# Mixture-of-experts block on one core: two-block and one-block expert rounds take turns

## What is computed

```python
logits = hf @ w_router + b_router
top_vals, top_idx = lax.top_k(logits, 4)          # 1024 tokens, 32 experts
weights = softmax(top_vals)
...
def expert_block(args):                           # one block: up to 128 tokens of one expert
    x_i, e = args
    gu = x_i @ w_gate_up[e] + b_gate_up[e]        # 1024 -> 2048
    gate, up = jnp.split(gu, 2, axis=-1)
    gate = jnp.minimum(gate, 7.0)
    up = jnp.clip(up, -7.0, 7.0)
    act = (up + 1.0) * (gate * jax.nn.sigmoid(1.702 * gate))
    return act @ w_down[e] + b_down[e]            # 1024 -> 1024
```

## Time and profile before

| | |
|---|---|
| median of 3 runs | 3197.2 us (3193.49 to 3198.83) |
| the profiled execution | 3199.73 us, span 3198.2 us |
| TensorE matmul busy | 2709.4 us, 85% |
| VectorE busy | 2038.1 us, 64% |
| ScalarE busy | 1532.5 us, 48% |
| mean granted TensorE clock | 0.927 of full |
| transfers | 685.50 MB, mean 214 GB/s |
| routing stage | from about 1093 to 1187 us |
| experts' stage | from about 1187 to 3104 us |

### The profile page before, as it was taken

One profiled execution on the slowest core, in us unless ns is written; L12 is line 12 of the kernel. 1 busy time (PEld: TensorE's weight loads), 2 busy tenths in 40 slices (PEclk: granted clock), 3 DMA queues, 4 the chain that ended last, 5 costly groups with the idle time before them and its releaser, 6 DMA issues. The chain is left out here.

```text
span 3198.2 us, 42791 instructions
## 1 busy us (share of the span) xinstructions
PE 2709.4 (85%) x12364; PEld 2128.5 (67%) x12365; DVE 2038.1 (64%) x3092; ACT 1532.5 (48%) x2203; POOL 271.1 (8%) x366
## 2 busy tenths in 40 slices
PE   1499979896789617999999999999999999999972
PEld 1388857674667516777777777777777777777750
DVE  6511034444553327867777896798678979787948
ACT  1212134342341106746555775587456757575721
POOL 0000011100000041111010111011001100010100
PEclk8699989997899758999999999999999999999985
DMA  8422132211342308957668896699668969886957
GB/s 338 168 102 76 47 101 80 70 50 56 104 148 97 133 28 274 357 209 247 225 233 295 300 367 225 235 367 346 211 210 280 368 223 367 292 301 231 356 194 262
DMA packets 450243, 685.50 MB, mean 214 GB/s; under 512 B 27473, under 2 KB 368865, under 8 KB 445825
## 3 DMA queue, kind: packets, MB, share of 16 engines
q1 hardware_dynamic: 420000, 591.83, 54.0%
q0 software_dynamic: 27872, 84.41, 7.3%
q10 hardware_dynamic: 2304, 8.39, 0.7%
HBM read 633.85 MB, written 59.60 MB: 217 GB/s over the span
## 5 line engine op out<-in xcount | busy, mean ns | idle before, releaser
L2034 DVE TENSOR_TENSOR e_gu_lo<-gu_raw,e_gu_hi 128x1024 fp32r<-128x1024 f32 x564 | 680.0, 1219 | 162.7 <-ACT e_gu_hi L1916 162.7
L78 PE MATMUL e_pgu<-e_gu_hi,e_x_hi 128*128 128x512 f32 x1568 | 643.3, 410 | 6.0 <-issue 6.0
L1916 ACT ACTIVATE e_gu_hi<-gu_raw 128x1024 fp32r<-128x1024 f32 x564 | 574.9, 1047 | 105.8 <-SPq L1740 82.9
L79 PE MATMUL e_pgu<-e_gu_lo,e_x_hi 128*128 128x512 f32 x1568 | 620.2, 396 | 0.0
L80 PE MATMUL e_pgu<-e_gu_hi,e_x_lo 128*128 128x512 f32 x1568 | 620.0, 395 | 0.0
L80 PEld LDWEIGHTS e_pgu<-e_gu_hi,e_x_lo 128*128 128x128 f32 x1568 | 294.9, 188 | 71.9
L78 PE MATMUL e_pdn<-e_dn_hi,e_a_hi 128*128 128x512 f32 x784 | 317.3, 405 | 26.0 <-DVE e_a_lo L2068 26.0
L78 PEld LDWEIGHTS e_pgu<-e_gu_hi,e_x_hi 128*128 128x128 f32 x1568 | 295.4, 188 | 65.9 <-issue 6.4
L2040 DVE TENSOR_TENSOR e_dn_lo<-dn_raw,e_dn_hi 128x1024 fp32r<-128x1024 f32 x280 | 333.0, 1219 | 4.5 <-ACT e_dn_hi L1922 4.4
L79 PEld LDWEIGHTS e_pgu<-e_gu_lo,e_x_hi 128*128 128x128 f32 x1568 | 295.9, 189 | 59.1
L80 PE MATMUL e_pdn<-e_dn_hi,e_a_lo 128*128 128x512 f32 x784 | 310.2, 396 | 0.0
(11 more groups left out here) (340 smaller groups left out, 4145.5 us busy)
## 6 DMA issues: line engine op xcount, KB each, us to landing
gu_raw<-in_w_gate_up_dram SPq DMA_DIRECT2D x572, 512.0 KB, 10.0
dn_raw<-in_w_down_dram SPq DMA_DIRECT2D x142, 1024.0 KB, 10.0
gu_bias<-in_b_gate_up_dram SPq DMA_DIRECT2D x141, 256.0 KB, 9.3
wada<-in_w_ada_dram SPq DMA_DIRECT2D x24, 1024.0 KB
c_y<-expert_rows SPq DMA_DIRECT2D x8, 2048.0 KB
win_raw<-in_w_in_dram POOLq DMA_DIRECT2D x6, 2048.0 KB, 8.8
proj_by_token<-out_stage SPq DMA_DIRECT2D x32, 256.0 KB, 2.0
wg_raw<-in_w_in_dram POOLq DMA_DIRECT2D x16, 512.0 KB, 4.8
```

The lines of the kernel that those rows point to most:

```text
L78: pe.matmul(out, a[0], w[0], start=first, stop=False)
L79: pe.matmul(out, a[0], w[1], start=False, stop=False)
L1916: act.activation(gu_hi[:, b, 2 * j:2 * j + 2], gu_raw[:, b, 2 * j:2 * j + 2].rearrange("p k g n -> p k (g n)"), ACT.Copy).then_inc(gu_hi_d ...
L2034: dve.tensor_tensor(gu_lo[:, b, 2 * j:2 * j + 2], gu_raw[:, b, 2 * j:2 * j + 2].rearrange("p k g n -> p k (g n)"), gu_hi[:, b, 2 * j:2 * j ...
```

## The change

The table is computed in another order: a round of two blocks and a round of one take turns as long as both are left, and then whatever is left follows. Expert 0's first round stays first, because its weights are already being loaded; `starts_double` says whether it has two blocks. Per expert, `c[:, 0]` is now its number of two-block rounds and `c[:, 1]` its number of one-block rounds (0 or 1); TensorE sums both over earlier experts and, in a second product, over all. `seen` is, per round, how many two-block rounds come before it. An expert that has both kinds no longer has them one behind the other. `phase_experts` is unchanged.

```diff
-        rid = sb(ctx, "r_rid", [NE, ROWS], F32)
-        ridi = sb(ctx, "r_ridi", [NE, ROWS], I32)
+        cum = sb(ctx, "r_cum", [NE, 8], F32)
+        rid = sb(ctx, "r_rid", [NE, ROWS + 1], F32)
+        ridi = sb(ctx, "r_ridi", [NE, ROWS + 1], I32)
...
-            c.step(pool.iota(ridi[:], [[1, ROWS]], base=0, channel_multiplier=0))
+            c.step(pool.iota(ridi[:], [[1, ROWS + 1]], base=0, channel_multiplier=0))
...
-            pe.matmul(pw[0:NE, 0:4], before[0:NE, 0:NE], cnt[:, 0:4], start=True, stop=True).then_inc(cummed, 1)
+            pe.matmul(pw[0:NE, 0:4], before[0:NE, 0:NE], cnt[:, 0:4], start=True, stop=True)
+            pe.matmul(pw[0:NE, 4:8], ones[0:NE, 0:NE], cnt[:, 0:4], start=True, stop=True).then_inc(cummed, 1)
...
-            v.step(dve.tensor_scalar(c[:, 5:6], c[:, 4:5], GROUP / 2 - 0.5, 1.0 / GROUP, ALU.add, ALU.mult))
+            v.step(dve.tensor_scalar(c[:, 5:6], c[:, 4:5], -0.5, 1.0 / GROUP, ALU.add, ALU.mult))
             v.step(dve.tensor_scalar(c[:, 6:7], c[:, 4:5], P / 2 - 0.5, 1.0 / P, ALU.add, ALU.mult))
             v.step(dve.tensor_copy(cnti[:, 0:2], c[:, 5:7]))
             v.step(dve.tensor_copy(c[:, 0:2], cnti[:, 0:2]))
-            v.step(dve.tensor_copy(c[:, 2:4], cnti[:, 0:2]))
+            v.step(dve.scalar_tensor_tensor(out=c[:, 1:2], in0=c[:, 0:1], scalar=-2.0, in1=c[:, 1:2], op0=ALU.mult, op1=ALU.add))
+            v.step(dve.tensor_tensor(c[:, 3:4], c[:, 0:1], c[:, 1:2], ALU.add))
+            v.step(dve.tensor_scalar(first[:], pid[:], 0.0, None, ALU.is_equal))
+            v.step(dve.scalar_tensor_tensor(out=c[:, 2:3], in0=c[:, 0:1], scalar=1.0, in1=first[:], op0=ALU.min, op1=ALU.mult))
             dve.sem_inc(cum_in, 1)
             dve.wait_ge(cummed, 1)
-            v.step(dve.tensor_copy(c[:, 4:6], pw[0:NE, 0:2]))
-            v.step(dve.tensor_tensor(c[:, 6:7], c[:, 4:5], c[:, 0:1], ALU.add))
-            v.step(dve.tensor_scalar(rh[:, 0], rid[:], c[:, 4:5], None, ALU.is_ge))
-            v.step(dve.tensor_scalar(rh[:, 1], rid[:], c[:, 6:7], None, ALU.is_lt))
-            v.step(dve.tensor_tensor(rh[:, 0], rh[:, 0], rh[:, 1], ALU.mult))
-            v.step(dve.tensor_scalar(rh[:, 1], rid[:], c[:, 4:5], None, ALU.subtract))
-            v.step(dve.tensor_scalar(rv[:, 0], rh[:, 0], pid[:, 0:1], None, ALU.mult))
-            v.step(dve.tensor_tensor(rv[:, 1], rh[:, 0], rh[:, 1], ALU.mult))
-            v.step(dve.tensor_scalar(rv[:, 2], rh[:, 0], c[:, 1:2], None, ALU.mult))
-            v.step(dve.tensor_scalar(rv[:, 3], rh[:, 0], c[:, 5:6], None, ALU.mult))
+            v.step(dve.tensor_copy(cum[:], pw[0:NE, 0:8]))
+            n_doubles, n_singles, starts_double = cum[:, 4:5], cum[:, 5:6], cum[:, 6:7]
+            v.step(dve.tensor_scalar(turn[:], rid[:], starts_double, 0.5, ALU.add, ALU.mult))
+            v.step(dve.tensor_scalar(turn[:], turn[:], 0.25, None, ALU.subtract))
+            v.step(dve.tensor_copy(turni[:], turn[:]))
+            v.step(dve.tensor_copy(turn[:], turni[:]))
+            v.step(dve.tensor_scalar(turn[:], turn[:], n_doubles, None, ALU.min))
+            v.step(dve.scalar_tensor_tensor(out=doubles[:], in0=rid[:], scalar=n_singles, in1=turn[:], op0=ALU.subtract, op1=ALU.max))
+            seen = doubles[:, 0:ROWS]
+            v.step(dve.tensor_tensor(kind[:, 0], doubles[:, 1:ROWS + 1], seen, ALU.subtract))
+            v.step(dve.tensor_scalar(kind[:, 1], kind[:, 0], -1.0, 1.0, ALU.mult, ALU.add))
+            v.step(dve.tensor_scalar(nth[:, 0], seen, cum[:, 0:1], None, ALU.subtract))
+            v.step(dve.scalar_tensor_tensor(out=nth[:, 1], in0=rid[:, 0:ROWS], scalar=cum[:, 1:2], in1=seen, op0=ALU.subtract, op1=ALU.subtract))
+            for j in range(2):
+                v.step(dve.scalar_tensor_tensor(out=rh[:, j], in0=nth[:, j], scalar=0.0, in1=kind[:, j], op0=ALU.is_ge, op1=ALU.mult))
+            for j in range(2):
+                v.step(dve.scalar_tensor_tensor(out=rh[:, j], in0=nth[:, j], scalar=c[:, j:j + 1], in1=rh[:, j], op0=ALU.is_lt, op1=ALU.mult))
+            v.step(dve.tensor_tensor(kind[:, 0], rh[:, 0], rh[:, 1], ALU.add))
+            v.step(dve.tensor_scalar(rv[:, 0], kind[:, 0], pid[:, 0:1], None, ALU.mult))
+            v.step(dve.tensor_tensor(nth[:, 0], nth[:, 0], rh[:, 0], ALU.mult))
+            v.step(dve.scalar_tensor_tensor(out=rv[:, 1], in0=rh[:, 1], scalar=c[:, 0:1], in1=nth[:, 0], op0=ALU.mult, op1=ALU.add))
+            v.step(dve.tensor_copy(rv[:, 2], rh[:, 0]))
+            v.step(dve.tensor_tensor(nth[:, 1], rid[:, 0:ROWS], seen, ALU.add))
+            v.step(dve.tensor_tensor(rv[:, 3], nth[:, 1], kind[:, 0], ALU.mult))
             dve.sem_inc(rows_in, 1)
...
-            v.step(dve.scalar_tensor_tensor(out=row2[:, 5], in0=row[:, 1], scalar=-2.0, in1=row[:, 2], op0=ALU.mult, op1=ALU.add))
-            v.step(dve.tensor_scalar(row2[:, 2], row2[:, 5], 2.0, None, ALU.is_ge))
-            v.step(dve.scalar_tensor_tensor(out=row2[:, 6], in0=row[:, 1], scalar=2.0, in1=row[:, 3], op0=ALU.mult, op1=ALU.add))
-            v.step(dve.tensor_scalar(row2[:, 3], row2[:, 6], 4.0, None, ALU.mult))
+            v.step(dve.tensor_copy(row2[:, 2], row[:, 2]))
+            v.step(dve.tensor_scalar(row2[:, 3], row[:, 3], 4.0, None, ALU.mult))
```

More of the change, by code:

```diff
@@ L1417, in phase_route @@
         cnti = sb(ctx, "r_cnti", [NE, 4], I32)
-        rid = sb(ctx, "r_rid", [NE, ROWS], F32)
-        ridi = sb(ctx, "r_ridi", [NE, ROWS], I32)
+        cum = sb(ctx, "r_cum", [NE, 8], F32)
+        rid = sb(ctx, "r_rid", [NE, ROWS + 1], F32)
+        ridi = sb(ctx, "r_ridi", [NE, ROWS + 1], I32)
+        turn = sb(ctx, "r_turn", [NE, ROWS + 1], F32)
+        turni = sb(ctx, "r_turni", [NE, ROWS + 1], I32)
+        doubles = sb(ctx, "r_doubles", [NE, ROWS + 1], F32)
+        kind = sb(ctx, "r_kind", [NE, 2, ROWS], F32)
+        nth = sb(ctx, "r_nth", [NE, 2, ROWS], F32)
+        first = sb(ctx, "r_first", [NE, 1], F32)
         pidi = sb(ctx, "r_pidi", [NE, 1], I32)
@@ L1508, in _ @@
                 ins = pe.matmul(ptab[0:1, j * ROWS:(j + 1) * ROWS], ones[0:NE, 0:1], rv[:, j], start=True, stop=True)
-            pe.matmul(ptab[0:1, 4 * ROWS:4 * ROWS + 1], ones[0:NE, 0:1], cnt[:, 0:1], start=True, stop=True).then_inc(rows_out, 1)
+            pe.matmul(ptab[0:1, 4 * ROWS:4 * ROWS + 1], ones[0:NE, 0:1], cnt[:, 3:4], start=True, stop=True).then_inc(rows_out, 1)
             for t in range(NT):
```

## The result

The changed kernel takes 3202.44 us (median of 20 runs, 3199.08 to 3207.06), the kernel before 3196.03 us (20 runs, 3192.23 to 3202.94): a ratio of 1.002 with a 95% interval of 1.0013 to 1.0027. That is 6.4 us more (4.2 to 8.6). 5.6 were forecast, and 3202.8 us.

What follows compares the result with a forecast made beforehand. TensorE was taken to bound two-block rounds, with VectorE and transfers both nearly full in one-block rounds. Routing +3.1 and rounds with end +2.5 gave +5.6 us (3.4 to 6.9), so 3202.8 us, range 3198 to 3209.

Steps and rivals of the forecast that it cites:

- The table: Routing stage: VectorE's longer serial chain delays the list positions and everything behind them, +3.1 us, bounds 1.6 to 3.7.
- The order of the rounds: Expert rounds: known transition lengths summed, end 0.5 us earlier by markers, some 0.8 us later for TensorE, bounds 0.4 to 1.2.
- The end of the last round: Last down projection: copy 7.9 us behind the marker, not 5.2; with order and clock +2.5 us, bounds 1.8 to 3.2.
- 0.3 for the clock: Last 12 matmuls: TensorE idle longer ahead of them, clock lower, +0.3 us, bounds 0 to 0.8.
- No gain from turns: Expert rounds: VectorE does all 24 weight pieces of a one-block round whatever was fetched, so S after D gains nothing.
- Seven singles fall behind: Rival, tail of one-block rounds: transfers fall behind, rounds five to seven 2.1 us longer each, +6.4, 3209 us; chance 0.06.
- The double's spare transfers help: Rival, one-block rounds after two-block ones: early weights cut them to 36.0 us, −31 us, 3172 in all; chance 0.04.
- The order does not change what runs: Rival, table: comes out in the old order, leaving only routing's 3.1 us, 3200.3 us; chance 0.03.
- The chain or the end costs more than its rows say: Rival, routing steps or last scatter: 1.5 to 3 us more, 3205.5 us, deciding 0.9 above the sum; chance 0.17.
- The rule weighed: HBM limit near 358 GB/s: one-block rounds transfer-bound at 42.0 us, fewer S after S give back 5.4, sum about +0.2.

Runs made afterwards that it cites:

- changed, again: The changed kernel itself, unaltered, run for a second profiled execution: 3204.22 us, span 3202.7.
- the moved block: Kernel before, old order, with VectorE's list positions made ahead of the table: 3190.92 us, ratio 0.9975.
- the idle steps: Kernel before, old order, with 12 unneeded serial VectorE steps added ahead of `rows_in`: 3201.02 us against 3198.23, ratio 1.001.
- the positions first and the new order: Changed kernel with VectorE's list positions made ahead of the table: 3193.57 us, ratio 0.9982 to the kernel before.
- surplus rounds ahead: Changed kernel with the seven surplus one-block rounds ahead of the turns, last round two-block: 3204.33 us, ratio 1.0015 to the kernel before.
- the sorted order: Changed kernel's table with all 21 one-block rounds first, then the 14 two-block rounds: 3196.46 us, ratio 0.9996 to the kernel before.
- the runs that relieve one side at a time: VectorE making half the gate/up low parts: turns 3169.53 us, sorted 3183.29; kernel before loading half of each down-projection chunk: 3195.64 against 3194.23.
- the sorted kernel with VectorE relieved: Sorted order, one-block rounds first, with VectorE making the low part of only half of each gate and up piece: 3183.29 us, span 3181.7.

## Why the prediction was right

The mechanism held in all three terms: a longer chain on the path, rounds that keep the lengths of the earlier trace rows, a dearer end. Three profiles side by side show how the terms came out, in us:

| stretch | before | changed | changed, again | forecast of the difference |
|---|---|---|---|---|
| end of the counting products to end of the positions' cast | 11.4 | 14.6 | 14.6 | +3.1 |
| positions to TensorE's first gate-and-up product | 78.5 | 75.1 | 75.8 | 0 |
| that product to ScalarE's last copy | 1875.9 | 1881.7 | 1878.5 | +2.5 |
| last copy to the first load of the last stage | 12.8 | 12.6 | 12.6 | 0 |

Single profiles agree with the forecast partly by luck. In the first, the stretches that were forecast at 0 come to −3.4 and −0.2, and the stages ahead of the table and behind the experts, which no row here shows, to −0.3 and +1.5; together −2.4, they offset most of the 3.3 us by which the third row exceeds its forecast. The median, 3202.44 against 3202.8, is as close because the base of three runs was 1.2 us too high and the difference 0.8 too small; the forecast itself is the difference, 5.6 against 6.4.

**The table.** +3.1 us forecast, +3.15 measured. The price per step from the earlier trace rows held: the three-operand step that the trace of before did not show took 0.26 us, next to 0.24 for its nearest kin. That the chain is on the path is shown by the moved block (−8.0 us), and in size by the idle steps (+3.2).

**The order of the rounds.** The transitions had the lengths of the earlier trace rows to a few hundredths in all orders tried, but for the rounds named above. (The 0.8 us that the prediction gives the order are 5 times 0.17 by its own rows, 73.38 against 73.21, and not 0.1.) The second profile's +2.6 for rounds and end together meets the 2.5. The first has 5.8, of which some 3 are its two clock falls (41.78 − 39.76 and 42.35 − 41.12, and 0.2 given back in the round behind each).

**The end of the last round.** The mechanism was right, and the size was nearly so, because two errors partly cancel. The copy came 8.6 and 8.1 us behind the marker's place, where 7.9 and 0.3 for the clock were forecast. VectorE's last low part ended 2.8 us behind it in both, 0.2 sooner than forecast. From the first of the 12 last products to the copy it took 5.6 and 5.1 us, against 4.7 before: the clock cost 0.9 and 0.4, where 0.3 was forecast with a bound of 0.8. Of the 11 distances between these products, seven were those of the lower level (0.43, the first 0.59) before, nine in the changed kernel's second profile and all in its first. That the longer idle stretch ahead of them does this is not shown. With the positions first and the new order TensorE waits 4.55 us there too, and only six distances are slow (4.5 us to the copy); with surplus rounds ahead and with the sorted order it waits 1.9 us, and all eleven are. The 0.3 was a small term whose reason the runs do not bear out.

**No gain from turns.** The reason given, that VectorE does all its pieces in the round whatever has been fetched, is shown by the runs that relieve one side at a time. The one-block round is held at 41.12 us by VectorE; relieve VectorE, and behind another one-block round the transfers hold it at some 41.0, and only then does a two-block round ahead save anything. The gain that turns seem to promise was never on the path.

**The rivals.** Seven singles fall behind: out, with 21 in a row. The double's spare transfers help: out for this kernel, right for one whose VectorE has less to do. The order does not change what runs: out, by the markers. The chain or the end costs more than its rows say: the timing does not exclude it, since it begins 0.9 us above the sum and the median lies 0.8 above; the traces do for the chain (3.15 us) and leave it some tenths at the end (0.4 us over the forecast in the first profile, 0.1 under in the second).

The rule weighed with them is out too: the runs hold 364 to 367 GB/s over whole one-block rounds, 364 where the transfers set the pace. The Trainium skill, DMA: Bandwidth & Descriptors, section Bandwidth, gives about 358 GB/s a core where both cores of a pair stream, and 425 for a core alone in a transfer of 16 MB. With one core at work here, the rounds are faster than the 358 would let them be, and the 425 was not reached over a round.

What the timing leaves open is the last microsecond: 6.4 us measured and 5.6 forecast differ by less than the interval of the ratio (4.2 to 8.6 us). The two falls of the clock and the late weight ahead of one of them, some 3 us in the first profile, are in no term of the forecast, and how often they come in the 20 runs is not known.

## What to carry to other kernels

Before rounds or tiles of different kinds are put in another order, read the length of each kind behind each neighbour that the trace already shows. If a pair is as long together as apart, the spare of one does not reach the other, and the sum of those windows is the forecast. Two limits can lie on top of each other (here VectorE and the transfers at 41 us), so a full DMA row does not prove that transfers bind: relieve one limit at a time to see. And when a table for a later stage is computed in the same queue as something that another engine waits for, put that something first: 8 us here, more than any order of rounds gave.

## What the runs showed of the hardware

TensorE's granted clock fell to its lower level for 3.4 us inside a steady loop that is at the upper level nearly always: 0 to 2 times per execution, four times in the nine profiles with full work. Three of the four falls came within 1.2 us behind an idle stretch of TensorE of 2.19 us, where 1.79 is usual, and each time ScalarE had waited for a late weight 12 us before; the fourth came behind a stretch of 1.80 us. The other one-block rounds of these profiles, over 180, have 1.8 us at that place, and but for the fourth no fall. So a stretch of 2.19 us went with a fall each time, but it is not needed for one; and in the sorted kernel with VectorE relieved a stretch of 2.4 us at another place of the round passes without a fall (1819 to 1941 us, granted clock 1.00). The four rounds were 1.2 to 2.0 us longer in all, of which 0.2 came back in the next round. A difference of a few microseconds between two single profiles of this kernel can be just that, or the 73.5 to 78.5 us from the list positions to the first product.
